# One tile's expert gates scattered into zeroed DRAM instead of built from one-hot matmuls, and the selection reached 11 expert blocks earlier

## The reference, cut to what matters

```python
def peer(xn, wq, subkeys, u_tab, v_tab):
    q = (xn @ wq).reshape(bsz, s, PEER_HEADS, 2, PEER_HALF)          # 8 heads, 2 halves of 128
    sub = jnp.einsum('bshpd,hpnd->bshpn', q, subkeys)                # 128 scores a half
    s_top, i_top = lax.top_k(sub, PEER_TOPK)                         # best 16 of 128
    cand = s_top[..., 0, :, None] + s_top[..., 1, None, :]
    best, pos = lax.top_k(cand, PEER_TOPK)                           # best 16 of the sums
    expert = ...                                                     # i * 128 + j of 16384 experts
    gate = jax.nn.softmax(best, axis=-1)
    a = jax.nn.gelu(einsum('td,ted->te', xb, u_tab[expert]))         # 8 * 16 experts a token
    y = einsum('te,ted->td', gate * a, v_tab[expert])
```

## Time and profile before

| what | us |
|---|---|
| median of 3 runs (2195.1 to 2200.02) | 2197.84 |
| the profiled execution's own time | 2191.74 |
| its span in the profile | 2190.0 |
| PE busy | 2142.9 |
| DVE busy | 1477.7 |
| ACT busy | 886.4 |
| POOL busy | 856.1 |

### The profile page before, as it was taken

How to read it: one execution, slowest core, us unless ns; L and a number is a source line. 1 busy time by engine, 2 the same in 40 slices (tenths; PEclk the granted TensorE clock), 3 DMA queues, 4 the chain that set the end, 5 groups by cost and what they waited for, 6 DMA issues and landing times.

```text
span 2190.0 us, 29584 instructions
## 1 busy us (share of the span) xinstructions
PE 2142.9 (98%) x10879; PEld 1864.9 (85%) x10879; DVE 1477.7 (67%) x2763; ACT 886.4 (40%) x1341; POOL 856.1 (39%) x450
## 2 busy tenths in 40 slices
PE   7989999999999999999999999999998999999999
PEld 6757888888877877899999999999997888888887
DVE  5973411110146994346879999999767999999887
ACT  5355422232253444343334555555433333333332
POOL 1003244444333433345667422222343455434452
PEclk9999999999999999999999999999999999999999
DMA  5302233333342322344444899997799999999996
GB/s 176 97 7 65 93 97 97 97 98 87 92 121 68 88 67 86 97 138 135 132 136 147 269 307 295 302 290 260 255 358 333 374 372 380 376 374 365 375 351 256
DMA packets 222219, 444.10 MB, mean 203 GB/s; under 512 B 83803, under 2 KB 133884, under 8 KB 221948
## 3 DMA queue, kind: packets, MB, share of 16 engines
q1 hardware_dynamic: 119612, 291.20, 39.5%
q0 software_dynamic: 36864, 134.23, 17.2%
q10 hardware_dynamic: 65600, 16.78, 3.4%
HBM read 397.71 MB, written 44.43 MB: 202 GB/s over the span
## 4 chain that ended last, share of the span: by engine, by line
PE 87%; DVE 7%; ACT 2%; DMA 2%; issue 1%; POOL 1%; SPq 0%; DVEq 0%; ACTq 0%; POOLq 0%
PE bank L449 26%; PE bank L452 26%; PE bank L453 26%; PE bank L930 4%; DVE cacc L1734 1%; DMA wraw<-in_peer_u 1%; DVE m L1927 1%; PE bank L899 1%; POOL WL L1110 1%; DVE xn L1928 1%; PE bank L621 1%; ACT sc L1250 1%; ACT WH L1139 0%; PE bank L836 0%; DMA wraw<-in_w_in 0%
## 5 line engine op out<-in xcount | busy, mean ns | idle before, releaser
L1110 POOL TENSOR_TENSOR WL<-wraw,WH 128x1024 fp32r<-128x1024 f32 x182 | 467.7, 2575 | 736.7 <-ACT WH L1139 736.7
L1139 ACT ACTIVATE WH<-wraw 128x1024 fp32r<-128x1024 f32 x411 | 435.2, 1060 | 619.1 <-PE bank L449 341.0
L449 PE MATMUL bank<-XH,WH 128*128 128x384 f32 (+2 forms) x1864 | 668.4, 359 | 12.3 <-DVE WL L2236 5.2
L452 PE MATMUL bank<-XL,WH 128*128 128x384 f32 (+2 forms) x1864 | 657.9, 353 | 0.0
L453 PE MATMUL bank<-XH,WL 128*128 128x384 f32 (+2 forms) x1864 | 657.9, 353 | 0.0
L449 PEld LDWEIGHTS bank<-XH,WH 128*128 128x128 f32 x1864 | 352.0, 189 | 44.2 <-issue 11.2
L452 PEld LDWEIGHTS bank<-XL,WH 128*128 128x128 f32 x1864 | 352.0, 189 | 28.5 <-issue 0.7
L453 PEld LDWEIGHTS bank<-XH,WL 128*128 128x128 f32 x1864 | 351.4, 189 | 28.5
L2236 DVE TENSOR_TENSOR WL<-wraw,WH 128x1024 fp32r<-128x1024 f32 x229 | 279.6, 1222 | 105.5 <-ACT WH L1139 98.9
L1118 POOL DMA_INDIRECT y<-in_peer_u_rows,gidx x128 | 182.1, 1423 | 356.8 <-DVE gdot L2247 346.3
L449 PE MATMUL bank<-WH,GH 128*128 128x512 f32 x768 | 299.2, 390 | 1.9 <-issue 1.6
(11 more groups left out here) (304 smaller groups left out, 2577.9 us busy)
## 6 DMA issues: line engine op xcount, KB each, us to landing
wraw<-in_peer_u SPq DMA_DIRECT2D x128, 512.0 KB
wraw<-in_peer_v SPq DMA_DIRECT2D x128, 512.0 KB
activations<-ac SPq DMA_DIRECT2D x122, 192.0 KB
ar<-activations SPq DMA_DIRECT2D x122, 192.0 KB
gate_matrices<-Gs ACTq DMA_DIRECT2D x4, 4096.0 KB, 35.7
gr<-gate_matrices SPq DMA_DIRECT2D x128, 128.0 KB
wraw<-in_w_gate SPq DMA_DIRECT2D x22, 512.0 KB
wraw<-in_w_up SPq DMA_DIRECT2D x22, 512.0 KB
```

The lines of the kernel that those rows point to most:

```text
L449: mm = pe.matmul(out, wh, xh, start=first, stop=False)
L452: pe.matmul(out, wh, xl, start=False, stop=False)
L1110: pool.tensor_tensor(WL[:, u % NW, 0:m], wraw[:, u % NR, 0:m], WH[:, u % NW, 0:m].bitcast(F32), ALU.subtract).then_inc(s("w_lo"), 1)
L1139: act.activation(WH[:, u % NW, 0:k * n], wraw[:, u % NR, 0:k * n], ACT.Copy).then_inc(s("w_hi"), 1)
```

## The change

Tile 0 (128 of the 384 dense tokens, `TSCAT`) no longer has its gates built by PE. SP writes zeros to those tokens' part of `gate_matrices`, 16 DMAs of 512 KB in runs of 256 bytes, one at every fourth weight unit from `("wg", 4)` of the first block's feed-forward on. When the choice is done, DVE works out the address of each gate (three short instructions), and POOL adds the gates into DRAM with 128 indirect DMAs of 128 elements of 4 bytes (`scatter`, with `compute_op` add), two behind each of the first 64 row gathers; every 16th waits until all before it have landed. 64 fours are left, one for each of the 64 blocks.

`UP_BY_PART` goes from 2 to 1 and `UP_BEFORE_SEL` from 10 to 15, so that `FIRST_GATE_UP` is 32 instead of 43 and there are 32 blocks behind the last four instead of 21. `sub(hp)` comes right behind the block of its own projection. The first four loads for the down stage are spread over blocks 120, 122, 124 and 126.

```diff
+TSCAT = P
+FIRST_FOUR = TSCAT // TOK4
-UP_BY_PART = 2
-UP_BEFORE_SEL = 10
+UP_BY_PART = 1
+UP_BEFORE_SEL = 15
+SCAT_PER_ROW = 2
+ZRUN = 64
+ZBLOCKS = 8
-EXPS_AFTER = 2 * PH * UP_BY_PART + 6
-LOAD_AT = NEXP - 4
+EXPS_AFTER = FIRST_GATE_UP - 5
+LOAD_AT = NEXP - 2 * NAG
...
 def fours_of(x):
-    return range(b * NFOUR // GATE_UPS, (b + 1) * NFOUR // GATE_UPS)
+    fours = NFOUR - FIRST_FOUR
+    return range(FIRST_FOUR + b * fours // GATE_UPS, FIRST_FOUR + (b + 1) * fours // GATE_UPS)
...
# PE
                 by_halves(3, [(("wq", hp), ("q2", hp)) for hp in range(2)])
+                subkeys()
                 for hp in range(2 * PH):
                     if hp >= 2:
                         tile(("wq", hp), ("q2", hp))
-                    if hp:
-                        sub(hp - 1)
                     for x in range(hp * UP_BY_PART, (hp + 1) * UP_BY_PART):
                         tile(("u", x), ("a", x), tokens=TD)
-                    if hp == 0:
-                        subkeys()
-                sub(2 * PH - 1)
+                    for p in (0, 1) if hp == 0 else () if hp == 1 else (hp,):
+                        sub(p)
...
-                        for t in range(NTD):
+                        for t in range(TSCAT // P, NTD):
                             out = take("sel", t)
...
# SP, among the weight units of the first block
+                if u >= unit_at[("wg", 4)] and (u - unit_at[("wg", 4)]) % 4 == 0 and u < unit_at[("wg", 4)] + 4 * (NEXP // ZBLOCKS):
+                    if u == unit_at[("wg", 4)]:
+                        sp.wait_ge(s("zeros_made"), 1)
+                    half, x = (u - unit_at[("wg", 4)]) // 4 % 2, (u - unit_at[("wg", 4)]) // 8 * 2 * ZBLOCKS
+                    sp.dma_start(gd[x:x + 2 * ZBLOCKS, :, half * ZRUN:(half + 1) * ZRUN].rearrange("x p t -> p x t"),
+                                 zeros[:, :].unsqueeze(1).to_broadcast([P, 2 * ZBLOCKS, ZRUN])).then_inc(
+                                     s("zeroed"), 16)
...
# SP, among the up blocks
-                            for tt in range(NGT - NGSTAY):
+                            sp.wait_ge(s("scattered"), 16 * HS)
+                            for tt in range(TSCAT // GTOK, NGT - NGSTAY):
                                 sp.wait_ge(s(f"g_out{tt}"), 16)
-                            for n in range(NAG):
-                                load_weighing(n)
+                        if x >= LOAD_AT and (x - LOAD_AT) % 2 == 0:
+                            load_weighing((x - LOAD_AT) // 2)
...
# POOL
+            def scatter(k):
+                if k == 0:
+                    pool.wait_ge(s("scatter_made"), 1)
+                    pool.wait_ge(s("zeroed"), 16 * (NEXP // ZBLOCKS))
+                elif k % SEL == 0:
+                    pool.wait_ge(s("scattered"), 16 * k)
+                pool.indirect_dma_start(out=gate_cells[:, :],
+                                        out_offset=bass.IndirectOffsetOnAxis(ap=scat_at[:, k:k + 1], axis=0),
+                                        in_=scat_gate[:, k:k + 1], in_offset=None, compute_op=ALU.add).then_inc(
+                                            s("scattered"), 16)
...
                                         ).then_inc(s(f"row_landed{row % NGATHER}"), 16)
+                for k in range(min(row * SCAT_PER_ROW, HS), min((row + 1) * SCAT_PER_ROW, HS)):
+                    scatter(k)
...
# DVE, behind the choice
+                expert = step(dve.scalar_tensor_tensor(out=scat_expert[:, :], in0=sel[:, 0, 0, :], scalar=float(N_KEYS),
+                                                       in1=sel[:, 1, 0, :], op0=ALU.mult, op1=ALU.add))
+                dve.tensor_copy(scat_gate[:, :], sel[:, 2, 0, :])
+                dve.wait_ge(s("own_row_made"), 1)
+                dve.wait_ge(s("dve_link"), expert)
+                dve.scalar_tensor_tensor(out=scat_at[:, :], in0=scat_expert[:, :], scalar=float(TSTAY),
+                                         in1=own_row[:, 0:1].to_broadcast([P, HS]), op0=ALU.mult, op1=ALU.add).then_inc(
+                                             s("scatter_made"), 1)
```

More of the change, by code:

```diff
@@ L251, in block_pair_kernel @@
         rt = sb("rt", [P, T])
+        with ExitStack() as under:
+            scat_at = sb("scat_at", [P, HS], U32, under)
+            scat_gate = sb("scat_gate", [P, HS], F32, under)
+            scat_expert = sb("scat_expert", [P, HS], F32, under)
         rstd = sb("rstd", [P, T])
@@ L261, in block_pair_kernel @@
         iota128 = sb("iota128", [P, P], F32)
+        own_row = sb("own_row", [P, 1], F32)
         VROWS = [("mix_pre", KD), ("ffn_pre", KD), ("norm1", KD), ("norm2", KD),
@@ L330, in block_pair_kernel @@
             m8 = sb("m8", [P, 8], F32, sc)
+            zeros = sb("zeros", [P, ZRUN], F32, sc)
         pflat = pT2[:, :, :, :].rearrange("p a b c -> p (a b c)")
@@ L407, in block_pair_kernel @@
         gain_row = xn[:, :, :].rearrange("p a n -> p (a n)")
+        gate_cells = gd.rearrange("x p (t a) -> (x p t) a", a=1)
         u_rows = A["peer_u_rows"]
@@ L926, in up_and_gates @@
                         out = take("gm", four)
-                        pe.wait_ge(s("hots_made"), four + 1)
+                        pe.wait_ge(s("hots_made"), four - FIRST_FOUR + 1)
                         q = four % NQ
@@ L1093, in _ @@
                       allow_small_or_imprecise_dtypes=True).then_inc(s("iota_made"), 1)
+            pool.iota(own_row[:, :], pattern=[[1, 1]], base=0, channel_multiplier=1,
+                      allow_small_or_imprecise_dtypes=True).then_inc(s("own_row_made"), 1)
+            pool.memset(zeros[:, :], 0.0).then_inc(s("zeros_made"), 1)
             for u, (k, n, _) in enumerate(units[:LOW_BY_DVE]):
@@ L1521, in choose_experts @@
                         act.activation(qq[:, p % 2, :], src[:, :], ACT.Copy).then_inc(frees(("q2", p)), 1)
[L1522 to L1525, removed]
                     if hp == 0:
@@ L1530, in choose_experts @@
                                            ACT.Copy).then_inc(frees(("sk", q)), 1)
-                sub(2 * PH - 1)
+                    for x in range(hp * UP_BY_PART, (hp + 1) * UP_BY_PART):
+                        activate(x)
+                    for p in (0, 1) if hp == 0 else () if hp == 1 else (hp,):
+                        sub(p)
             def activate(x):
@@ L1563, in copy_gates @@
                 tt, at = four // per, four % per * TOK4
-                if at == 0 and tt >= 2:
+                if at == 0 and tt >= TSCAT // GTOK + 2:
                     act.wait_ge(s(f"g_out{tt - 2}"), 16)
@@ L2264, in hots_of @@
                     for four in fours_of(x):
-                        if four >= NQ:
+                        if four >= FIRST_FOUR + NQ:
                             wait_full(dve, ("gm", four - NQ))
```

## The result

The changed kernel takes 2239.54 us (median of 5 runs, 2236.05 to 2242.66), the kernel before 2197.84 us (5 runs): ratio 1.019, 95% interval 1.0175 to 1.0205. It is slower by 42 us, where 25 us less were forecast. What happened is rival 1, POOL as the pace, which had been worked out at 2232 us and given 0.27.

A forecast was written before the change was run, and what follows sets the result against it. PE was taken as the bound, busy 2142.9 of 2190.0 us. Work removed -28.8, the choice +1 and waits behind the fours +3 gave -25 us: 2173 us on the median, range 2166 to 2180.

The forecast's parts named there:

- rival 1: POOL becomes the pace: rows too slow, so DVE and then PE wait; 2232 us at 5.94 us a row; chance 0.27.
- POOL, the engine that gets the new work: POOL's gather and two scatters per row: 1.49 us per DMA, 4.6 to 4.7 us a row with landings; fits.
- The 0.26: Mean us that DVE's L2247 and L2236 hold up each POOL DMA, added to 0.93 us; L2268 was not counted.
- the limit of 5.0 us: Time POOL may take per row, from about 1161 us to row 63, before PE feels it.
- PE's saving: Work removed from PE: 32 of 96 fours, 28.5 us, and three selection transposes, 0.3 us; 28.8 us in all.
- The whole change but the scatters: The forecast sum, with the scatters priced as fitting on POOL: -25 us.
- The choice: At the selection: index ready at about 1158.5 us, 4 us before PE asks at 1162.9; stage priced at 1 us.
- Rival 2: The choice comes late: PE waits 5 to 10 us at the selection, 2181 us; chance 0.10.
- Behind the fours: Last up blocks, 32 instead of 21 without fours: PE waits 8.4 us for low halves, 3 more than before.
- The zeros: 16 stores of 512 KB among the first feed-forward's weight loads: covered, price 0; without cover at most 72 us.
- Landings: Every eighth row POOL waits for 16 scatters to land: 2.1 us, of which the next gather covers 1.2.

The follow-up runs named there:

- plain write: The changed kernel with all 128 scatters writing instead of adding, so gates are lost where two heads of a token choose the same expert: 2194.49 us.
- one a row (64): The changed kernel with one scatter behind each of the first 64 gathers, half of tile 0's choices left out: 2175.12 us.
- spread, all: The changed kernel with all scatters, seven per five gathers, fours over 86 blocks, one gather a block, 16 blocks before the selection, later down-stage loads: 2176.28 us.
- spread, three in two, all: The "spread, all" kernel with three scatters to two gathers and the fours over 82 blocks: 2184.67 us.
- three in two (96): The changed kernel with three scatters per two of the first 64 gathers, a quarter of tile 0's choices left out: 2187.97 us.
- the order alone: The changed kernel with all 96 fours by PE, no zeros or scatters: 2202.82 us with 15 blocks before the selection, 2194.92 us with 16.
- The old order: The changed kernel, scatters kept, with UP_BY_PART back at 2 and UP_BEFORE_SEL at 10: 2236.77 us.

## Why the prediction was wrong

**The step that failed** is the price of a scatter in "POOL, the engine that gets the new work". I took the gather as its nearest row: 0.93 us, and 0.26 for what DVE holds up, 1.19. It takes 1.85 in the mean. With nothing of DVE's beside it, a scatter with the add takes 1.56 us, so 0.63 of the 0.66 us that are missing are this base price; the plain write's is 0.97, so the base price is the add's. What DVE holds up is the other 0.29. The gather was 1.37 instead of 1.19. Twice 0.66 and once 0.18 are the 1.5 us between 4.6 and 6.09. The forecast had a margin of 0.3 us a row, and its price rested on a DMA without arithmetic.

**The 0.26 was near only by luck.** I wrote that a DMA beside L2268 is not held up, and counted L2236 and L2247 alone. The trace before already had two gathers that began under L2268, and both waited for its end. The first pair of lines is one of them, the second a scatter of the changed kernel, where L2268 is L2311:

```profile
1218.04 1.22 DVE L2268 TENSOR_TENSOR hots<-iota,sq 128x1024 f32<-128x1024 f32 x1
1218.39 1.68 POOL L1118 DMA_INDIRECT y<-in_peer_u_rows,gidx  x1 [1.10 <-DVE gdot L2247]
1193.87 1.22 DVE L2311 TENSOR_TENSOR hots<-iota,sq 128x1024 f32<-128x1024 f32 x1
1193.99 2.55 POOL L1143 DMA_INDIRECT gate_matrices<-scat_gate,scat_at  x1 [0.30 <-issue]
```

The gather ends 0.81 us behind DVE's instruction, the scatter 1.45 us. Of the 128 scatters of the changed kernel 31 began under L2311, and they have 21.8 of the 37 us by which all scatters exceed 1.56 us each. In the plain write 50 of 128 did, and they have 45 of 60 us; that is why its mean lies 0.47 us over its shortest.

**The mechanism of rival 1 was right**, and so was its limit: 63 x (6.09 - 5.0) = 69 us, less 25, is 44 us slower, and 42 were measured. That its 5.94 us a row and 2232 us came so close is in part luck, since it took one price, the gather's median of 1.68, for all three DMAs, and they were 1.85 twice and 1.37. Here are the kernels by their row, with the limit of 5.0 us (4.82 and 4.86 where the fours are spread):

| kernel | scatters to a gather | us a row | us |
|---|---|---|---|
| without scatters | 0 | - | 2171.6 |
| one a row (64) | 1 | 4.71, of which POOL needs 3.7 | 2175.1 |
| spread, all | 1.4 | 4.85 | 2176.3 |
| spread, three in two, all | 1.5 | 5.02 | 2184.7 |
| three in two (96) | 1.5 | 5.22 | 2188.0 |
| plain write, all | 2 | 5.45 | 2194.5 |
| the change | 2 | 6.09 | 2239.5 |

Up to the limit a scatter is all but free, beyond it every 0.1 us costs 5 to 8 us. The chance of 0.27 was low for a kind of DMA that the trace lacked, and for which the range of the trace's own rows, 0.93 to 1.98 us, reached far over the limit.

**PE's saving** of 28.8 us was about right: 31.2 between the two kernels that differ in it. **The whole change but the scatters** was forecast at -25 us and came to -26. Some of that is luck: the 4 us that I set against the saving were 1 for the choice and 3 for the waits behind the fours, and the 5 us that the order alone lost went with a wait at the selection.

**The choice** was mis-sized. It was to be ready at 1158.5 us, 4 us before PE asks, and was ready at 1169.3; PE asked at 1165.3 and waited 4.0 us. The first ranking began at 950.73, 2.2 us later than I had it. DVE's work from there on is 210 us, not 200, and 6.8 us of it are the two kinds of instruction that the last section shows. Rival 2 thus came true in small, beside rival 1. Its price is 8 us in the order alone.

**Behind the fours** I forecast 8.4 us of waits for low halves; without the scatters they are 3.8 us in all. **The zeros** cost nothing, as forecast: PE begins to transpose the keys at 943.24 us in the changed kernel, which stores them, and at 946.29 and 944.82 in the two of the order alone, which don't. **Landings**, forecast at about 1 us for each of eight waits, were 7.2 us in six. **The old order** with the scatters is 2.8 us from the new one, so the new order is not what the loss comes from.

What stays open: the six runs with 96 scatters lie at 2181.5 to 2183.7 and at 2192.2 to 2193.5 us, three each. The row is close to the limit there, but no run shows what tips it. Open, too, is the price of the wait at the selection, 8 us in one pair of kernels and 2 to 4 in another.

## What to carry to other kernels

Before work goes to an engine with idle time, ask for the time between two uses of what it delivers in that stretch: POOL was busy for 39% of the span, and still had no more than 5.0 us for each row. If the work doesn't fit there, spread it before dropping it; a version with the same 128 scatters over 92 rows instead of 64, and with the fours and gathers thinned out to match, turned 42 us lost into 21 gained. And where a margin is 6% and the new operation is in no row of the trace, the forecast is about that operation, and should be made with the wide end of the bounds as its first case. Before an instruction is called harmless, look up the rows in which it stands beside the new one: two were enough here.

## What the runs showed of the hardware

**An indirect DMA with an add costs the issuing engine more.** POOL spends at least 1.55 us on 128 elements with the add, 0.97 without, and 0.93 on a gather of 128 rows of 4 KB. So 4 bytes an element or 4 KB a row made no difference to POOL here, and the add did.

**A DMA that POOL begins under some of DVE's instructions waits for their end.** In the changed kernel L2279, L2290 and L2311 hold it up, each with two inputs of 128x1024: a scatter with the add ends 1.45 us behind them, a gather 0.88. L2315, of 128x512, does not: 20 scatters began under it and took 1.60 us in the mean.

**POOL and DVE lock each other out for a whole instruction.** DVE's instruction with two inputs of 128x2048 took 2.27 to 2.29 us in all 8 cases before. In the changed kernel (ns min/median/max), then its timeline with POOL's subtraction of the low half beside it:

```profile
L2205 DVE TENSOR_TENSOR hot<-hot,itf x8: 2269/2349/4489, 1002.7 to 1160.9; 128x2048 f32<-128x2048 f32 x8
1140.62 2.29 DVE L2196 TENSOR_TENSOR hot<-bhf,iota 128x2048 f32<-128x2048 f32 x1
1141.88 3.29 POOL L1132 TENSOR_TENSOR WL<-wraw,WH 128x1024 fp32r<-128x1024 f32 x1 [1.77 <-ACT WH L1175]
1156.30 2.39 POOL L1132 TENSOR_TENSOR WL<-wraw,WH 128x1024 fp32r<-128x1024 f32 x1 [2.92 <-ACT WH L1175]
1156.36 4.49 DVE L2196 TENSOR_TENSOR hot<-bhf,iota 128x2048 f32<-128x2048 f32 x1
```

The later one stands still until the earlier one ends. DVE's at 1156.36 begins 0.06 us behind POOL's, which ends at 1158.69, and it ends 2.16 us after that. POOL's at 1141.88 meets DVE's, which ends at 1142.91, and takes 3.29 us instead of 2.39. Three of DVE's sixteen two-input instructions of this size took 4.4 to 4.5 us, all of them behind the last query; before, none of sixteen was held up. It is not the constants of the new order that do it: with the old ones and the scatters seven of sixteen took 4.37 to 4.40 us, from 1041 us on, and DVE's work up to the index was 224 us. Nor do the scatters or the zeros, since the order alone, without both, has three and, with 16 blocks, two of them. All these kernels let the scores follow the blocks of their own query, and the kernel before does not. That this moved DVE's instructions under POOL's subtractions is argued, not shown. The Trainium skill (SBUF — State Buffer, "Who interferes with whom") has a DVE instruction with two inputs in SBUF contend with an instruction of GpSimd that reads SBUF; the trace agrees, with 2.29 us that become 4.49.

**Behind a short wait of PE the clock is lower.** In the changed kernel the six transposes behind the 4.0 us wait take 426 ns in the mean, where the nine before took 272, and the 40 us window with them has a granted clock of 0.91. It is 0.91 in the order alone with its 4.0 us wait, too, and 0.96 in the kernel without scatters, with the same wait:

```profile
L933 PE MATMUL bank<-ident,sel 128*128 128x128 f32 x6 | 1.5, 426 | 4.0 <-DVE sel L2211 4.0
```

It is lower as well where PE waits often: the changed kernel has 33 waits for low halves, the longest 4.5 us, and the stretch from 1240 to 1580 has 0.97. Two of the three kinds of matmul of 128x384 behind 1165 us take 343 ns in the mean there, where they take 335 without the scatters. Whether the many short waits or the few longer ones lower it is not shown.
